# Recurrent stage of a hybrid decoder layer on one core: two of five token chunks stored in the other half of the partitions, their products issued in pairs over all four quarters of the array

## The chip, the core and the metric

The kernel runs on 1 core of one Trainium2 chip. The metric is the device time in microseconds (us). Before the change it is 2426.48 us, the median of 3 runs (2426.11 to 2426.84).

## What is computed

One inference step of one decoder layer in fp32, for a prompt of 256 tokens and 8 samples of 8 tokens (320 tokens in all), width 2048. Three branches work side by side (a recurrent "RWKV-7" mixing, a gated spatial mixing, an attention over a memory), are merged by gates, and a gated MLP follows. The change touches the recurrent branch alone. For each of 16 heads of 64 channels the reference runs, token by token:

```
def step(S, inp):
    r_t, w_t, k_t, v_t, av_t, bv_t = inp
    sa = jnp.einsum('bhvk,bhk->bhv', S, av_t)
    S = S * w_t[:, :, None, :] + sa[..., None] * bv_t[:, :, None, :] + v_t[..., None] * k_t[:, :, None, :]
    return S, jnp.einsum('bhvk,bhk->bhv', S, r_t)
S, ys = lax.scan(step, wkv0.astype(f32), seq)
```

Then the output of each head is normalised, a bonus term is added, and the sum is multiplied by a gate.

## The kernel before

TensorE (PE) spends nearly all of its time on dense products with weights: for each unit of 1 MB of weights, ScalarE (ACT) makes a rounded copy (`hi_unit`, L211), VectorE (DVE) the rest (`lo_unit`, L218), and PE multiplies both with the 320 tokens (`pe_group_steps`, L246, L247, L255). SyncE brings in the units.

The recurrence is computed in chunks of 64 tokens: chunks 0 to 3 are the prompt, chunk 4 (`NCK`) holds the 8 samples. `wkv_pe`, `wkv_dve` and `wkv_act` loop 8 times (two calls of 4 iterations), and each iteration handles two heads: head 0 in partitions 0 to 63, head 1 in partitions 64 to 127. Such an iteration is a chain of small products with names in the table `PR`: `A`, `B`, `Cb`, `Bk`, `Ck` (chunk by chunk products of tokens with tokens), `beT`, `vT`, `kaT`, `alT` (a chunk turned so that its tokens lie in the partitions), `A2` to `QT4` (powers of a triangular matrix), `Z0` to `Z3` (their application), `X4`, `G`, `S0` to `S4`, `X` (states of the chunks), and the output `y` in bank 6. Each name gets one of three PSUM banks in turn (`RING = (4, 5, 7)`), so a product waits in `begin` until the result three names before it has been moved out. DVE moves most of them (semaphore `ring_out`), ACT the turned ones (`turned_out`).

A product of a chunk is two fp32 matmuls of 64x64, one for each head, from `heads`: head h reads partitions 64h to 64h+63 and writes the same ones, so it uses one diagonal quarter of the 128x128 array. The trace shows each fp32 matmul as two records. Tokens in the partitions always lie in the half of their head.

The dense products of the gates and of the branches are cut into 48 steps of 6 matmuls per iteration, and a table `STEPS` says how many are issued in front of which small product: they cover the time in which DVE and ACT work on the result before. `"A": 8` puts 8 steps in front of `A`, `Y_STEPS = 3` more stand in front of `y`. `UNIT_END` tells ACT after which product a weight unit has been used up.

DVE works in program order. `Prog.do` makes it wait for the end of each of its own instructions. Its order in an iteration is: masks on `A` to `Cb`, copies and sums for `A2` to `Z3`, `prepare_logs` (four instructions for the next iteration), `X4`, `G`, the products `sam` and `vtm` (with `m_e8`), the states (`state(c)`, L970), parts of the branches (`branch`, L1783 and L1787), the normalisation of the next iteration's keys (a reciprocal, L833), the copy of `y` (L989), the output's normalisation, and between them six `lo_unit`.

Of the kernel before, what the change touches and what calls it, by code (L numbers as in the profile page):

```python
# [35 lines left out]
CH = 64  # L36
# [72 lines left out]
def hybrid_step(nc, A, O):  # L109
    ctx = ExitStack()  # L110
    with ctx:
# [600 lines left out]
        st_ = [qr[:, 1920 + 64 * c:1984 + 64 * c] for c in range(NCK)]  # L712
# [49 lines left out]
        def wkv_pool(pool, pp):  # L762
# [53 lines left out]
        def prepare_logs(dve, vv, j):  # L816

            dve.wait_ge(S("low_out"), 2 * j + 2)
            vv.do(dve.tensor_scalar(ldx, ldx, -0.5 * C_DECAY, -0.5 * C_DECAY, ALU.mult, ALU.add))
            vv.do(dve.tensor_tensor_scan(cum, m_sc[:, :], ldx, 0.0, ALU.mult, ALU.add))  # L820
            vv.do(dve.tensor_tensor(ldx, cum, ldx, ALU.subtract), "logs")
            vv.do(dve.tensor_scalar(av, av, 0.5, 0.5, ALU.mult, ALU.add))
# [33 lines left out]
        def wkv_start_dve(dve, vv, beside):  # L856
# [13 lines left out]
            prepare_logs(dve, vv, 0)  # L870
            beside.due(AT_STEP["wq"] + 8)
# [21 lines left out]
        def wkv_dve(dve, vv, n):  # L893
            u = U_BR[n]
            with vv.loop(4 * n, 4 * n + 4, PER_V) as i:
# [12 lines left out]
                def masked(o, name, m, sem="ring_out"):  # L908
                    ps(name)
                    m = m[:, :, :] if len(m.shape) == 3 else bmid(m[:, :], NC)  # L910
                    tt(c5(o), c5(pbank(name)[:, 0:T]), m, ALU.mult, sem)

# [15 lines left out]
                tt(c5(t_bo)[:, 0:NCK], c5(pbank("B")[:, 0:T])[:, 0:NCK], bmid(m_bo[:, :], NCK), ALU.mult, "ring_out")  # L928
                ps("beT")
                vv.do(dve.tensor_copy(zc3[:, :, 0:64], c5(pbank("beT")[:, 0:T])), "ring_out")  # L930
                ps("Cb")
                tt(zc3[:, :, 64:128], c5(pbank("Cb")[:, 0:T]), m_in[:, :, :], ALU.mult, "ring_out")
# [3 lines left out]
                masked(t_bk, "Bk", m_st)  # L936
# [3 lines left out]
                masked(t_ck, "Ck", m_in)  # L940
# [27 lines left out]
                def state(c):  # L968
                    ps(f"S{c}")
                    vv.do(dve.tensor_scalar(st_[c], pbank(f"S{c}")[:, 0:64], pend_p[:, c:c + 1], None, ALU.mult), "ring_out")  # L970

                state(0)
                prepare_k(dve, vv, i + 1)
                state(1)
                branch(0, 0)
                state(2)
# [4 lines left out]
                state(3)  # L981
                branch(0, 1)
                ps("X")
                tt(t_x[:, 64:TP], t_x[:, 64:TP], pbank("X")[:, 0:192], ALU.add, "ring_out")
# [33 lines left out]
        PER_V = {"dve": 23, "kk_sq": 1, "logs": 1, "ring_out": N_OUT, "rk_ready": 1, "ops_ready": 1,  # L1018
# [7 lines left out]
        def prepare_act(act, aa, j, ps=None, beside=None):  # L1026
# [3 lines left out]
            if ps:  # L1030
                i = j - 1
                for name, dst, n in (("vT", v_t, T), ("kaT", ka_t, T), ("s0t", qr[:, 896:1408], 512), ("alT", alp_t, 192)):
                    ps(name)
                    aa.do(act.activation(dst[:, 0:n], pbank(name)[:, 0:n], ACT.Copy), "turned_out")
# [36 lines left out]
        def wkv_act(act, aa, n):  # L1071
            with aa.loop(4 * n, 4 * n + 4, {"low_out": 2, "exps": 3, "kk_root": 1, "v_copied": 1, "gn_sqrt": 1, "turned_out": N_OUT_A}) as i:
# [37 lines left out]
        def wkv_pe(pe, n):  # L1110
            u, t = U_BR[n], T_BR[n]
            for i in range(4 * n, 4 * n + 4):
# [18 lines left out]
                def begin(name, *needs):  # L1131

                    p = PR[name]
                    assert p == done[0], name
                    for _ in range(STEPS.get(p, 0) - (Y_STEPS if name == "g" else 0)):
# [40 lines left out]
                def turned(name, src, chunks=range(NC)):  # L1176
                    o = begin(name)
                    for n, c in enumerate(chunks):
                        for h in range(2):
                            r = slice(64 * h, 64 * h + 64)  # L1180
                            last = pe.matmul(o[r, 64 * n:64 * n + 64], src[r, 64 * c:64 * c + 64], m_id[r, :], start=True, stop=True)  # L1181
                    end(last)
# [25 lines left out]
                each("B", be, alp)  # L1208
                turned("beT", be)
                each("Cb", be, rh)  # L1210
                each("A2", t_bd, t_ad, ("Cb",))
                each("B2", t_ad, t_bd)
                each("Bk", ka, alp)
                wait("v_copied", i + 1)
                turned("vT", v_)
                each("RT1", t_b2, t_rt, ("B2",))
                each("B4", t_a2, t_b2)
                each("Ck", ka, rh)
                turned("kaT", ka)
# [14 lines left out]
                turned("alT", alp, range(1, NCK))  # L1234
# [13 lines left out]
                o = begin("G", "Z3")  # L1248
                for c in range(1, NCK):
                    last = heads(ch(o, c - 1), [(ch(alp_t, c - 1), zb(c))])  # L1250
                end(last)

                def state(c):
                    o = begin(f"S{c}", f"S{c - 1}" if c else "G")
                    end(heads(o[:, 0:64], [(zb(c), ch(t_x, c)), (ch(ka_t, c), ch(v_t, c))] + ([(ch(step_, c - 1), st_[c - 1])] if c else [])))

                state(0)
                state(1)
                state(2)
                o = begin("S4")  # L1260
                wait("sam_ready", i + 1)
                end(heads(o[:, :], [(zb(NCK), sam.rearrange("p b v -> p (b v)")), (ch(ka_t, NCK), vtm.rearrange("p b v -> p (b v)"))]))
                state(3)
                o = begin("X", "S2")
                for c in range(1, NCK):
                    last = heads(ch(o, c - 1), [(ch(alp, c), st_[c - 1])])
                end(last)
                for _ in range(Y_STEPS):
                    next(steps, None)
                wait("ring_out", OUT0 + N_OUT * i + 1 + OUT["X"])  # L1270
                wait("gated_out", i + 1)
                for c in range(NC):
                    terms = [(ch(t_x, c), zcb(c)), (ch(v_t, c), ch(t_ck, c))]
                    if 0 < c < NCK:
                        terms.append((st_[c - 1], ch(rh, c)))
# [1289 lines left out]
```

## Time and profile before

| what | value |
|---|---|
| median of 3 runs | 2426.48 us |
| span of the profiled execution, first to last instruction | 2425.4 us |
| instructions in it | 48608 |
| PE busy | 2375.4 us (98%) |
| PE weight loads busy | 2272.1 us (94%) |
| DVE busy | 1467.3 us (60%) |
| ACT busy | 893.6 us (37%) |
| GpSimd busy | 130.5 us (5%) |
| mean granted TensorE clock | 0.996 of full speed |

The profiled execution's own time is its span of 2425.4 us and some 1.1 us around it, which gives the median. Engines overlap, so their busy times don't add up. A matmul's record lasts from its start to the landing of its result, and records overlap: how long a product holds PE is read from the start of one product to the start of the next. The granted clock is 1.00 in all stretches of the recurrent stage, which is 2.4 GHz.

### The profile page before, as it was taken

Reading aid. Unit: us, or ns where it says so; the run is one execution under the profiler, and the core shown is the slowest. Engines: PE = TensorE matmul, PEld = TensorE weight load, DVE = VectorE, ACT = ScalarE, POOL = GpSimd, SP = SyncE. Lnnn points to the kernel's source line nnn. Section 1 sums busy time; section 2 is a strip of 40 time slices with the busy share of each in tenths; the row PEclk is TensorE's granted clock in tenths of the full one; section 3 lists DMA queues with packets and bytes.
Section 4 is the critical chain, followed back from the end, with each engine's and each line's share of the span. In section 5 each row is a group of like instructions: output and inputs, shape, how many; then the busy total and the mean of one; then the engine's idle time right before and its main releaser. Section 6 shows DMA issues by size and latency. Waiting matters only on the chain.

```text
span 2425.4 us, 48608 instructions
## 1 busy us (share of the span) xinstructions
PE 2375.4 (98%) x19598; PEld 2272.1 (94%) x19598; DVE 1467.3 (60%) x2060; ACT 893.6 (37%) x1038; POOL 130.5 (5%) x200
## 2 busy tenths in 40 slices
PE   8999999999999999999999998999999999999998
PEld 6899999898988888888999988999999999999998
DVE  5645444555677666776544446666666666566576
ACT  6433344343333333332434344333333333333334
POOL 3000001000000010000000011000000000000003
PEclk9999999999999999999999999999999999999999
DMA  7544486342333233322444632444444444444443
GB/s 266 192 155 152 152 292 238 103 140 84 96 99 95 92 126 100 97 87 93 143 149 151 201 121 88 157 155 138 156 156 142 152 154 140 143 159 148 156 139 109
DMA packets 282189, 346.67 MB, mean 143 GB/s; under 512 B 6957, under 2 KB 240733, under 8 KB 280907
## 3 DMA queue, kind: packets, MB, share of 16 engines
q1 hardware_dynamic: 272315, 308.44, 39.1%
q0 software_dynamic: 9712, 36.30, 4.6%
q8 instruction: 104, 1.70, 0.3%
q14 instruction: 26, 0.21, 0.0%
q10 hardware_dynamic: 32, 0.01, 0.0%
HBM read 333.83 MB, written 10.89 MB: 142 GB/s over the span
## 4 chain that ended last, share of the span: by engine, by line
PE 86%; DVE 8%; issue 3%; ACT 2%; DMA 1%; DVEq 0%; SPq 0%; ACTq 0%
PE bank L246 20%; PE bank L255 20%; PE bank L247 20%; PE bank L1165 5%; PE bank L227 4%; PE bank L228 4%; PE bank L229 4%; DVE work L906 1%; ACT hi L211 1%; DVE lo L218 1%; PE bank L1181 1%; PE bank L511 1%; DVE q L833 1%; PE bank L512 1%; PE bank L518 1%
## 5 line engine op out<-in xcount | busy, mean ns | idle before, releaser
L218 DVE TENSOR_TENSOR lo<-raw,hi 128x2048 fp32r<-128x2048 f32 x286 | 655.8, 2293 | 505.9 <-ACT hi L211 479.7
L246 PE MATMUL bank<-ah,hi 128*128 128x320 f32 x3200 | 958.1, 313 | 0.2 <-DVE al L532 0.2
L247 PE MATMUL bank<-al,hi 128*128 128x320 f32 x3200 | 945.8, 309 | 0.0
L211 ACT ACTIVATE hi<-raw 128x2048 fp32r<-128x2048 f32 x286 | 548.0, 1916 | 926.3 <-PE bank L255 678.6
L246 PEld LDWEIGHTS bank<-ah,hi 128*128 128x128 f32 x3200 | 600.8, 188 | 13.1 <-issue 9.8
L247 PEld LDWEIGHTS bank<-al,hi 128*128 128x128 f32 x3200 | 601.1, 188 | 0.4
L255 PE MATMUL bank<-ah,lo 128*128 128x320 f32 x3200 | 547.5, 311 | 0.0
L255 PEld LDWEIGHTS bank<-ah,lo 128*128 128x128 f32 x3200 | 487.2, 188 | 4.0 <-issue 0.8
L227 PE MATMUL bank<-bh,hi 128*128 128x320 f32 x704 | 218.7, 311 | 0.2 <-DVE work L2279 0.2
L229 PE MATMUL bank<-bh,lo 128*128 128x320 f32 x704 | 217.5, 309 | 0.0
L228 PE MATMUL bank<-bl,hi 128*128 128x320 f32 x704 | 217.5, 309 | 0.0
L1165 PE MATMUL bank<-work 64*64 64x64 f32 (+2 forms) x3680 | 166.0, 236 | 5.4 <-DVE work L906 4.3
L1165 PEld LDWEIGHTS bank<-work 64*64 64x64 f32 x3680 | 134.0, 134 | 35.8 <-issue 24.6
L227 PEld LDWEIGHTS bank<-bh,hi 128*128 128x128 f32 x704 | 132.2, 188 | 0.6 <-issue 0.6
L228 PEld LDWEIGHTS bank<-bl,hi 128*128 128x128 f32 x704 | 132.2, 188 | 0.0
L229 PEld LDWEIGHTS bank<-bh,lo 128*128 128x128 f32 x704 | 132.1, 188 | 0.0
L2279 DVE TENSOR_TENSOR work<-work,bank 128x320 f32<-128x320 f32 x176 | 85.6, 487 | 56.7 <-PE bank L229 47.1
L246 PE MATMUL bank<-bh,hi 128*128 128x320 f32 x384 | 118.0, 320 | 0.0
L2253 DVE SCALAR_TENSOR_TENSOR rw<-rw,prm 128x336 f32<-128x336 f32 x176 | 100.2, 569 | 22.2 <-DVE rw L2251 1.4
L247 PE MATMUL bank<-bl,hi 128*128 128x320 f32 x384 | 113.6, 309 | 0.0
L906 DVE TENSOR_TENSOR work<-work,bank 128x512 f32<-128x512 f32 (+3 forms) x56 | 28.9, 517 | 97.6 <-PE bank L1165 95.7
L246 PEld LDWEIGHTS bank<-bh,hi 128*128 128x128 f32 x384 | 72.1, 188 | 2.3
(372 smaller groups left out, 2036.2 us busy)
## 6 DMA issues: line engine op xcount, KB each, us to landing
raw<-in_w_in SPq DMA_DIRECT2D x98, 1024.0 KB, 5.2
raw<-in_w_up SPq DMA_DIRECT2D x88, 1024.0 KB, 5.1
raw<-in_w_down SPq DMA_DIRECT2D x44, 1024.0 KB, 5.1
raw<-in_w_branch SPq DMA_DIRECT2D x24, 1024.0 KB, 5.4
raw<-in_w_out SPq DMA_DIRECT2D x16, 1024.0 KB, 5.6
raw<-in_w_mem_k SPq DMA_DIRECT2D x8, 1024.0 KB, 5.6
raw<-in_w_mem_v SPq DMA_DIRECT2D x8, 1024.0 KB, 5.2
work<-in_cache_mem_k POOLq DMA_DIRECT2D x8, 1024.0 KB, 6.7
```

Source lines behind the costliest of these rows:

```text
L211: act.activation(hi[c % NS][:, :], raw[c % 2][:, :], ACT.Copy).then_inc(S("hi_done"), 1)
L218: dve.tensor_tensor(lo[c % NS][:, :], raw[c % 2][:, :], hi[c % NS][:, :], ALU.subtract)\
L227: pe.matmul(out, a_hi, b_hi, start=first, stop=False)
L228: pe.matmul(out, a_hi, b_lo, start=False, stop=False)
L229: return pe.matmul(out, a_lo, b_hi, start=False, stop=last)
L246: pe.matmul(out, w, xh[:, 8 * h + k, :], start=h + k == 0, stop=False)
L247: pe.matmul(out, w, xl[:, 8 * h + k, :], start=False, stop=False)
L255: last = pe.matmul(out, w, xh[:, 8 * h + k, :], start=False, stop=h == units - 1 and k == 7)
L906: vv.do(dve.tensor_tensor(o, a, b, op), sem)
L1165: last = pe.matmul(out[r, :], a[r, :], b[r, :], start=start and m == 0, stop=stop and m == len(pairs) - 1, **kw)
L2253: vv.do(dve.scalar_tensor_tensor(out=o, in0=x, scalar=w, in1=o, op0=ALU.mult, op1=ALU.add), "gate_conv" if j == 2 and q % 8 == 3 else None)
L2279: dve.tensor_tensor(f, f, bank[b][:, 0:T], ALU.add).then_inc(S(f"tile_out{b}"), 1)
```

## The change

It does these things, all inside the iteration of the recurrent stage:

- Chunks 0 and 1 (`TURNED`) keep tokens that lie in the partitions in the other head's half: head h has them in partitions 64(1-h) to 64(1-h)+63. A product that makes such a chunk reads head h's half and writes the other one, which is an off-diagonal quarter of the array. Chunks 2 to 4 (`UPRIGHT`) stay.
- Two products that don't depend on each other get two banks, one for the turned chunks and one for the upright ones, and are issued chunk by chunk in turn (`both`): `A` with `B` (`ABt`, `ABs`), `beT` with `Cb` (`beCt`, `beCs`), `Bk` with `Ck` (`BCt`, `BCs`), `vT` with `kaT` (`vkt`, `vks`).
- The states' two products that don't depend on the state before, and `G`, become one pair of banks, `St` and `Ss`. `S0` goes; `S1` to `S3` keep one product each, and DVE adds the rest, which it has stored scaled in `st_`. `X` gives its first chunk to a new `X1`.
- The terms of `y` for chunks 0 and 1 are issued between the halves of `S4`, whose matmuls are on the diagonal quarters.
- `alT` makes chunks 2 and 3 first, then 4 steps of dense work, then chunk 1, directly ahead of `Z2`.
- `bonus` comes first in the iteration. `prepare_logs` is cut in two (`prepare_shifted`), and `X4` stands ahead of it. The table `STEPS` names other products, with the same sum of 48.
- DVE moves each pair bank by bank. It issues 10 instructions more per iteration, ACT 2 more. PE has as many matmuls as before.

The diff, cut to its core:

```
+        TURNED = (0, 1)
+        UPRIGHT = (2, 3, 4)
-        for _n in ["A", "bonus", "B", "beT", "Cb", "A2", "B2", "Bk", "vT", "RT1", "B4", "Ck", "kaT", "RT2", "s0t",
-                   "Q", "QT", "Z0", "Z0s", "Q2", "QT2", "XB", "Z1", "QT4", "alT", "Z2", "z", "za", "ssq", "Z3", "X4", "G",
-                   "S0", "S1", "S2", "S4", "S3", "X", "g", "mean", "trp", "var", "tr0", "tr1"]:
+        for _n in ["bonus", "ABt", "ABs", "beCt", "beCs", "A2", "B2", "BCt", "BCs", "RT1", "B4", "vkt", "vks", "RT2", "s0t",
+                   "Q", "QT", "Z0", "Z0s", "Q2", "QT2", "XB", "Z1", "QT4", "alT", "Z2", "z", "za", "ssq", "Z3", "X4", "St", "Ss",
+                   "S1", "X1", "S2", "S4", "S3", "X", "g", "mean", "trp", "var", "tr0", "tr1"]:
...
-        STEPS = {"A": 8, "A2": 3, "RT1": 3, "RT2": 3, "Q": 3, "XB": 3, "Z2": 4, "Z3": 4, "S0": 2, "S1": 2, "S2": 2, "S3": 1, "X": 2,
+        STEPS = {"bonus": 8, "A2": 3, "RT1": 3, "RT2": 3, "Q": 3, "XB": 3, "alT": 4, "Z3": 4, "S1": 3, "S2": 3, "S3": 3,
                  "g": 5, "mean": 2, "var": 1}
-        Y_STEPS = 3
+        HELD = {"alT": 4, "g": 3}
...
-                masked(t_ad, "A", m_ad)
+                def part(o, name, at, chunks, m, sem=None):
+                    k = len(chunks)
+                    m = m[:, chunks[0]:chunks[0] + k, :] if len(m.shape) == 3 else bmid(m[:, :], k)
+                    tt(c5(o)[:, chunks[0]:chunks[0] + k], c3(pbank(name)[:, at:at + 64 * k]), m, ALU.mult, sem)
                 ps("bonus")
                 tt(bon, pbank("bonus")[:, 0:T], row_(i + 16), ALU.mult, "ring_out")
-                masked(t_bd, "B", m_bd, None)
...
+                for name, cs in (("ABt", TURNED), ("ABs", UPRIGHT)):
+                    k, states = 64 * len(cs), tuple(c for c in cs if c < NCK)
+                    ps(name)
+                    part(t_ad, name, 0, cs, m_ad)
+                    part(t_bd, name, k, cs, m_bd)
+                    part(t_bo, name, k, states, m_bo, "ring_out")
...
                 plus(zc, "Z3", 512)
-                prepare_logs(dve, vv, i + 1)
                 ps("X4")
                 tt(t_x[:, TP:T], t_x[:, TP:T], pbank("X4")[:, 0:64], ALU.add, "ring_out")
-                ps("G")
-                tt(c3(step_), c3(pbank("G")[:, 0:192]), bmid(m_id[:, :], NCK - 1), ALU.add, "ring_out")
+                prepare_logs(dve, vv, i + 1)
+                ps("St")
+                tt(c3(st_all[:, 0:128]), c3(pbank("St")[:, 0:128]), bc(pend_p[:, 0:2], CH), ALU.mult)
+                tt(step_[:, 0:64], pbank("St")[:, 128:192], m_id[:, :], ALU.add, "ring_out")
+                ps("Ss")
+                tt(c3(st_all[:, 128:256]), c3(pbank("Ss")[:, 0:128]), bc(pend_p[:, 2:4], CH), ALU.mult)
+                tt(c3(step_[:, 64:192]), c3(pbank("Ss")[:, 128:256]), bmid(m_id[:, :], 2), ALU.add, "ring_out")
+                prepare_shifted(dve, vv, i + 1)
...
+                def into_chunk(o, a, b, c):
+                    for h in range(2):
+                        last = pe.matmul(o[half(h ^ (c in TURNED)), :], a[half(h), :], b[half(h), :], start=True, stop=True)
+                    return last
...
+                def both(turned, upright, a1, b1, a2, b2):
+                    t, s = begin(turned), begin(upright, ahead=1)
...
+                    one(s, a1, b1, 2, 0)
+                    one(t, a1, b1, 0, 0)
+                    one(s, a1, b1, 3, 1)
+                    one(t, a1, b1, 1, 1)
+                    one(s, a1, b1, 4, 2)
+                    one(t, a2, b2, 0, 2)
+                    one(s, a2, b2, 2, 3)
+                    end(one(t, a2, b2, 1, 3))
+                    one(s, a2, b2, 3, 4)
+                    end(one(s, a2, b2, 4, 5))
...
+                y_terms(0, 0, start=True)
+                heads(o[:, :], [(zb(NCK), sam_)], stop=False)
+                y_terms(0, 1)
+                y_terms(1, 0)
+                y_terms(1, 1)
+                end(heads(o[:, :], [(ch(ka_t, NCK), vtm_)], start=False))
```

Where the order of instructions moves, it is shown from the built programs. First PE at the start of an iteration; the rows name the PSUM bank that is written and what is multiplied, `ops_ready`, `rk_ready` and `ring_out` are semaphores of DVE, `turned_out` of ACT. Before:

```order
L255 MATMUL bank3<-ah,lo0 128x320 x8
L1165 MATMUL bank4<-work 64x64 [waits ops_ready,turned_out,ring_out]
L1165 MATMUL bank4<-work 64x64 x9
L1207 MATMUL bank5<-work,head_ones 128x320 [waits rk_ready,turned_out,ring_out]
L1165 MATMUL bank7<-work 64x64 [waits turned_out,ring_out]
L1165 MATMUL bank7<-work 64x64 x9
L1181 MATMUL bank4<-m_id,work 64x64 [waits ring_out]
L1181 MATMUL bank4<-m_id,work 64x64 x9
L1165 MATMUL bank5<-work 64x64 [waits ring_out]
L1165 MATMUL bank5<-work 64x64 x9
```

With the change:

```order
L255 MATMUL bank3<-ah,lo0 128x320 x8
L1256 MATMUL bank4<-work,head_ones 128x320 [waits rk_ready,turned_out,ring_out]
L1208 MATMUL bank7<-work 64x64 [waits turned_out,ring_out,ops_ready]
L1208 MATMUL bank7<-work 64x64
L1208 MATMUL bank5<-work 64x64 x2
L1208 MATMUL bank7<-work 64x64 x2
L1208 MATMUL bank5<-work 64x64 x2
L1208 MATMUL bank7<-work 64x64 x2
L1208 MATMUL bank5<-work 64x64 x2
L1208 MATMUL bank7<-work 64x64 x2
L1208 MATMUL bank5<-work 64x64 x2
L1208 MATMUL bank7<-work 64x64 x4
L1208 MATMUL bank5<-m_id,work 64x64 [waits ring_out]
L1208 MATMUL bank5<-m_id,work 64x64
L1208 MATMUL bank4<-m_id,work 64x64 x2
```

`bonus` (with `head_ones`) has moved to the front, and the second pair, which writes banks 5 and 4, waits for `ring_out`: its bank 5 is that of `ABt`, from the pair before it.

Then DVE around the first states; `bank7` with 128x512 is the sum of `Z3`, the two rows with `m_e8` are `sam` and `vtm`. Before:

```order
L906 TENSOR_TENSOR work<-work,bank7 128x512 [waits wkv_ps]
L819 TENSOR_SCALAR work<-work 128x320 [waits low_out]
L820 SCALAR_TENSOR_TENSOR work<-m_scan,work 128x320 [waits dve]
L821 TENSOR_TENSOR work<-work 128x320 [waits dve]
L822 TENSOR_SCALAR rw<-rw 128x320 [waits logs]
L906 TENSOR_TENSOR work<-work,bank4 128x64 [waits wkv_ps]
L906 TENSOR_TENSOR work<-bank5,m_id 128x192 [waits wkv_ps]
L906 TENSOR_TENSOR work<-work,m_e8 128x512 [waits turned_out]
L906 TENSOR_TENSOR work<-work,m_e8 128x512 [waits dve]
L970 TENSOR_SCALAR q<-bank7,q 128x64 [waits wkv_ps]
L827 TENSOR_SCALAR rw<-rw,prm 128x320
```

With the change:

```order
L913 TENSOR_TENSOR work<-work,bank7 128x512 [waits wkv_ps]
L913 TENSOR_TENSOR work<-work,bank4 128x64 [waits wkv_ps]
L823 TENSOR_SCALAR work<-work 128x320 [waits low_out]
L824 SCALAR_TENSOR_TENSOR work<-m_scan,work 128x320 [waits dve]
L913 TENSOR_TENSOR q<-bank5,q 128x128 [waits wkv_ps]
L913 TENSOR_TENSOR work<-bank5,m_id 128x64 [waits dve]
L913 TENSOR_TENSOR q<-bank7,q 128x128 [waits wkv_ps]
L913 TENSOR_TENSOR work<-bank7,m_id 128x128 [waits dve]
L827 TENSOR_TENSOR work<-work 128x320 [waits ring_out]
L828 TENSOR_SCALAR rw<-rw 128x320 [waits logs]
L913 TENSOR_TENSOR work<-work,m_e8 128x512 [waits turned_out]
L913 TENSOR_TENSOR work<-work,m_e8 128x512 [waits dve]
L989 SCALAR_TENSOR_TENSOR q<-bank4,q 128x64 [waits wkv_ps]
L913 TENSOR_TENSOR work<-work,bank5 128x64 [waits wkv_ps]
L833 TENSOR_SCALAR rw<-rw,prm 128x320
```

`X4` has moved ahead of the logs, the one row on `G` has become four on `St` and `Ss`, and the row of `X1` (bank 5, 128x64) follows the state of chunk 1.

## Rows read from the trace of the kernel before

**Rows 1.** The page, its head and first part: busy us (share of the span) xinstructions.

```profile
span 2425.4 us, 48608 instructions
PE 2375.4 (98%) x19598; PEld 2272.1 (94%) x19598; DVE 1467.3 (60%) x2060; ACT 893.6 (37%) x1038; POOL 130.5 (5%) x200
```

**Rows 2.** Busy time of the recurrent stage: PE, PEld, DVE, ACT, POOL, clock.

```profile
551.00:1162.00 611.00, 600.59 (x7604) 539.02 (x7603) 408.98 (x639) 198.38 (x224) 41.33 (x73) 1.00 0.31 96
```

**Rows 3.** The chain of waits, in time order: start us, us, what.

```profile
770.76 0.50 DVE work L906
771.39 0.78 PE bank L1298 x2
```

**Rows 4.** Timeline of PE: start us, us, line, out<-in, records, idle before and its releaser.

```profile
703.68 0.80 PE L1165 MATMUL bank<-work 64*64 64x64 f32 x20
...
710.12 1.97 PE L1165 MATMUL bank<-work 64*64 64x64 f32 x60
711.92 0.75 PE L1181 MATMUL bank<-m_id,work 64*64 64x64 f32 x20
...
715.44 1.96 PE L1165 MATMUL bank<-work 64*64 64x64 f32 x60
...
744.41 1.10 PE L1165 MATMUL bank<-q 64*64 64x64 f32 x32
745.36 0.56 PE L1165 MATMUL bank<-work 64*64 64x64 f32 x12
...
748.42 0.45 PE L1165 MATMUL bank<-work 64*64 64x64 f32 x8 [0.54 <-DVE work L906]
...
750.76 0.45 PE L1165 MATMUL bank<-work 64*64 64x64 f32 x8
...
766.96 0.81 PE L1284 MATMUL bank<-q 128*128 128x320 f32 x2
...
780.02 0.80 PE L1165 MATMUL bank<-work 64*64 64x64 f32 x20
```

**Rows 5.** Groups of PE by line, a line with column tiles of 32: busy us, mean ns.

```profile
L1703 PE MATMUL bank<-work,small 128*32 128x256 f32 x128 | 8.7, 385 | 0.0
```

**Rows 6.** Timeline of PE, two products that lie in different rows of the array.

```profile
738.37 0.53 PE L1239 MATMUL bank<-q 64*128 64x320 f32 x1
738.38 0.53 PE L1241 MATMUL bank<-q 64*128 64x320 f32 x1
```

**Rows 7.** Timeline of DVE, from the sum of Z3 to the copy of y.

```profile
744.62 0.69 DVE L906 TENSOR_TENSOR work<-work,bank 128x512 f32<-128x512 f32 x1 [2.54 <-PE bank L1165]
...
747.66 0.22 DVE L906 TENSOR_TENSOR work<-work,bank 128x64 f32<-128x64 f32 x1
748.01 0.36 DVE L906 TENSOR_TENSOR work<-bank,m_id 128x192 f32<-128x192 f32 x1
748.49 1.42 DVE L906 TENSOR_TENSOR work<-work,m_e 128x512 f32<-128x512 f32 x2
...
750.03 0.29 DVE L970 TENSOR_SCALAR q<-bank,q 128x64 f32<-128x64 f32 x1
...
753.82 0.28 DVE L970 TENSOR_SCALAR q<-bank,q 128x64 f32<-128x64 f32 x1 [0.65 <-PE bank L1165]
...
759.65 0.35 DVE L906 TENSOR_TENSOR work<-work,bank 128x192 f32<-128x192 f32 x1
...
766.41 0.49 DVE L989 COPY work<-bank 128x320 f32<-128x320 f32 x1
```

**Rows 8.** Timeline of DVE, the end of the iteration and the first mask of the next.

```profile
779.41 2.29 DVE L218 TENSOR_TENSOR lo<-raw,hi 128x2048 fp32r<-128x2048 f32 x1 [0.19 <-DVE rw L906]
781.61 0.49 DVE L906 TENSOR_TENSOR work<-bank,m_ad 128x320 f32<-128x320 f32 x1
```

**Rows 9.** Timeline of DVE, the copies after A2 and B2, and the sum after RT1.

```profile
710.97 1.10 DVE L915 COPY work<-bank 128x320 f32<-128x320 f32 x2 [1.64 <-PE bank L1165]
...
716.28 0.49 DVE L906 TENSOR_TENSOR work<-work,bank 128x320 f32<-128x320 f32 x1 [1.06 <-PE bank L1165]
```

More of the change, by code:

```diff
@@ L935, in wkv_dve @@
                 plain(t_b2, "B2")
-                masked(t_bk, "Bk", m_st)
+                for name, cs in (("BCt", TURNED), ("BCs", UPRIGHT)):
+                    ps(name)
+                    part(t_bk, name, 0, cs, m_st)
+                    part(t_ck, name, 64 * len(cs), cs, m_in, "ring_out")
                 weights_low(0)
@@ L1174, in each, with half, out_of_chunk, one @@
                     end(last)
[L1176 to L1182, printed above, removed]
+                def half(h):
+                    return slice(64 * h, 64 * h + 64)
+                def into_chunk(o, a, b, c):
+                    for h in range(2):
+                        last = pe.matmul(o[half(h ^ (c in TURNED)), :], a[half(h), :], b[half(h), :], start=True, stop=True)
+                    return last
+                def out_of_chunk(o, a, b, c, start=True, stop=True, **kw):
+                    for h in range(2):
+                        r = half(h ^ (c in TURNED))
+                        last = pe.matmul(o[half(h), :], a[r, :], b[r, :], start=start, stop=stop, **kw)
+                    return last
+                def both(turned, upright, a1, b1, a2, b2):
+                    t, s = begin(turned), begin(upright, ahead=1)
+                    if turned == "ABt":
+                        wait("ops_ready", i + 1)
+                    def one(o, a, b, c, n):
+                        return into_chunk(ch(o, n), ch(a, c), m_id if b is None else ch(b, c), c)
+                    one(s, a1, b1, 2, 0)
[8 more added lines that the diff above has]
+                    end(one(s, a2, b2, 4, 5))
                 def zb(c):
@@ L1233, in wkv_pe @@
                 each("QT4", t_ad, t_bd, ("QT2",), NCK)
-                turned("alT", alp, range(1, NCK))
+                o = begin("alT")
+                into_chunk(ch(o, 1), ch(alp, 2), m_id, 2)
+                into_chunk(ch(o, 2), ch(alp, 3), m_id, 3).then_inc(S("al_upright"), 1)
+                for _ in range(HELD["alT"]):
+                    next(steps, None)
+                wait("al_upright", i + 1)
+                end(into_chunk(ch(o, 0), ch(alp, 1), m_id, 1))
                 apply("Z2", t_bd, range(NCK), "Z1")
@@ L1247, in wkv_pe, with from_zb @@
                 end(heads(o[:, 0:64], [(alm[:, b, :], s0t[:, b, :]) for b in range(NB)]))
[L1248 to L1251, printed above, removed]
+                o_t, o = begin("St", "Z3"), begin("Ss", ahead=1)
+                wait("turned_out", OUT0_A + N_OUT_A * i + 1 + OUT_A["alT"])
+                def from_zb(o, c):
+                    return out_of_chunk(o, zb(c), ch(t_x, c), c, stop=False)
@@ L1267, in wkv_pe @@
                 end(last)
-                for _ in range(Y_STEPS):
+                for _ in range(HELD["g"]):
                     next(steps, None)
                 wait("ring_out", OUT0 + N_OUT * i + 1 + OUT["X"])
[L1271 to L1275, printed above, removed]
-                    heads(ch(bank[6], c), terms, stop=c < NCK, skip_group_check=c == NCK)
+                for c in UPRIGHT:
+                    for m in range(2):
+                        y_terms(c, m)
@@ L1277, in wkv_pe @@
+                for c in range(1, NCK):
+                    heads(ch(bank[6], c), [(st_[c - 1], ch(rh, c))], start=False, stop=False, skip_group_check=True)
                 for b in range(NB):
```

121 lines of the change are left out of this document (74 added, 47 removed).

## Prediction

> **What bounds the kernel now.** I read the page first: PE is busy for 98% of a span of 2425.4 us [rows 1], and for 600.6 of the 611 us in which the eight iterations of the recurrent stage run, at a granted clock of 1.00, so at 2.4 GHz [rows 2]. That looks like a stage in which every matmul saved is time saved. The chain of waits corrects it: in an iteration it runs over DVE from the sum of Z3 on, and returns to PE only at L1298, the product for the variance, which starts at 771.39 us when DVE's square (770.76 + 0.50) has ended [rows 3]. PE waits there for DVE, it waits 0.54 us for the state S0 behind DVE's logs [rows 4], and between these DVE waits only once for PE, 0.65 us in front of the third state [rows 7]. So the second half of an iteration already runs at DVE's pace, and the first half at PE's. An iteration takes 780.02 - 703.68 = 76.34 us [rows 4].
>
> **What a small product costs.** 60 records take 1.97 us and 20 take 0.80 [rows 4], so a record takes (1.97 - 0.80)/40 = 0.029 us, and a chunk's product (two heads, four records) 0.117 us: call it a round. Both heads' quarters work at once in it. Leaving dense work for small products and coming back costs a group of its own: from 748.42 to 750.76 lie 2 rounds and 12 dense matmuls, 2.34 - 0.23 = 2.11 us; from 710.12 to 715.44 lie 20 rounds and 18 dense ones, 5.32 - 2.34 = 2.98 us [rows 4]. So 6 dense matmuls are 0.87 us, and a group costs 2.11 - 12 x 0.145 = 0.37 us beside its rounds.
>
> **Do four quarters work at once?** No row has it. One bound: the pair takes as long as its records one after the other, 10 rounds. The other: turned chunks are hidden wholly beside upright ones, 6 rounds. Column tiles that read the same rows of the array do overlap: 128 records of 128x32 with 256 columns, 0.385 us each, keep PE busy for 8.7 us, 0.068 us each [rows 5]. Tiles in different rows that write the same columns start 0.01 us apart [rows 6]. A turned quarter shares rows with one upright quarter and columns with the other, and both kinds of sharing are shown to be harmless, so I take 6 rounds.
>
> **What PE saves.** Four pairs (AB, beC, BC, vk) at 4 rounds each are 16 rounds; G with the first two products of S0 to S3 is 11 rounds, St with Ss 6; the four terms of y for chunks 0 and 1 lie beside S4. That is 25 rounds, 2.93 us. Separate groups go from 15 to 12, 1.1 us. The wait for S0 goes, 0.54 us. In all some 4.5 us per iteration, 36 us in eight: what the change would bring if PE set the pace.
>
> **What DVE pays, and why it decides.** The second pair needs bank 5, which DVE must have emptied of ABt. In the kernel before, nothing in the first 60 records had such a wait behind late work. Behind the waiting pair stand its own products, 3 dense steps and A2, and everything of the iteration follows. So a loop closes: sum of Z3, DVE without a pause up to the masks of ABt in the next iteration, the pair beC on PE, and on to the next Z3. I sum it, since no iteration can be shorter.
>
> *DVE's part.* From 744.62 [rows 7] to the end of the last `lo_unit`, 779.41 + 2.29 = 781.70 [rows 8], are 37.08 us. Its wait of 0.65 shrinks to the ordinary 0.13 between instructions with a semaphore of PE (747.88 to 748.01) [rows 7]: 36.56. Removed: G, 0.48 (748.01 to 748.49); S0, 0.29 + 0.13; X goes from 192 columns, 0.35, to 128 [rows 7], which I put at 0.29, between 0.22 for 64 and 0.36 for 192. That is 0.96. Added: St 0.29 + 0.22, Ss 0.29 + 0.29, X1 0.22, with three waits of 0.13 and two gaps of 0.03, 1.76. X4 now follows Z3's sum at once: it lands at 744.41 + 1.10 = 745.51 [rows 4], 0.12 later than DVE could take it. Sum 37.48. Then bonus and the three masks of ABt: the first mask starts at 781.61 now [rows 8], 0.09 before the `lo_unit` ends; 0.49 + 0.13 + 3 x 0.29 + 2 x 0.03 = 1.55, less 0.09 is 1.46. DVE's part is 38.94 us. The exponentials of ACT get their logs 1.8 us later, because `prepare_shifted` stands behind Ss; ACT then has a root and a weight unit before DVE's fourth `lo_unit` needs it. I count that as just covered, with some 0.3 us left; if the cover is gone, DVE's part grows by what is late.
>
> *PE's part.* The pair beC, 6 rounds, and the dense steps to A2: 0.70 + 2.98 = 3.68. From A2 to the sum of Z3 it is 744.62 - 710.12 = 34.50 now [rows 4, 7]. BC and vk save 4 rounds each, the third chunk of alT lies beside Z2: 9 rounds, 1.05 less. Two waits are new. BCs needs bank 7 of A2: DVE starts that copy 0.85 us after A2's start and takes 0.49 [rows 9], so with 0.06 for the handover (y copied at 766.90 [rows 7], gate's product at 766.96 [rows 4]) and 0.05 for the weights the bank is free at 1.45, and B2 is through at 1.22: 0.23 lost. vks needs bank 4 of RT1. BC's products end 2.15 us after A2's start and its four masks at 3.64; the `lo_unit` behind them lets go of DVE at 6.05. RT1 itself starts at 5.09, and its sum could start 0.84 us later, at 5.93 (716.28 after 715.44 now [rows 4, 9]); so it runs from 6.05 to 6.54, the bank is free at 6.65 with handover and weights, and PE is through with B4 at 6.31: 0.34 lost. Sum 3.68 + 34.50 - 1.05 + 0.57 = 37.70.
>
> With 0.10 for the handover (0.06 there, 0.13 in rows 3) the loop is 38.94 + 37.70 + 0.10 = 76.74 us, 0.40 more than 76.34. It closes seven times in eight iterations: +2.8 us. Made against the profiled execution (2425.4 us, and 1.1 us around it, equal to the median) this gives 2426.5 + 2.8 = **2429.3 us**. All of PE's 4.5 us per iteration turn up as waits: about 2 us in front of beC, about 3 us in front of the gate's product, which waits for y's copy.
>
> **The rivals.**
> - *Slower: the quarters don't overlap.* If PE can't start records closer than now, 0.029 us on the mean in every row, a pair takes 10 rounds. beC, BC and vk lie in the loop: 12 rounds, 1.40 us, so 1.80 x 7 = 12.6 us, 2439.1 us. It decides from the point where a pair takes more than 7 rounds. For it: no stretch with small products is quicker. Against it: rows 5 and 6. Chance 0.15. The Trainium skill, "TensorE: Matmul & The Clock Gate", section "Wait — 56ns, not 53.3ns?", says that starts never come closer than about 25 ns; an estimate by it is 1.0 us for a pair's 40 records instead of 0.70, and 2435.6 us for the kernel. By that rule and by the mean of the rows alike this speaks against the change; the 0.01 us of rows 6 are single starts, which no mean disproves.
> - *Slower: DVE's or ACT's part is longer.* Ten instructions more, half of them behind a semaphore: 0.05 us more for each, or a fourth `lo_unit` that waits for ACT, make it 0.5 us more per loop: 0.9 x 7 = 6.3, 2432.8 us. Chance 0.20.
> - *Faster: the loop is looser than I count.* If the gaps of DVE shrink where results have long been ready, or waits go that I kept, the loop could be 1.2 us shorter than its sum, 75.5 us: 0.8 x 7 = 5.6 us less than now, 2420.9 us; if DVE were not in the way at all, 2426.5 - 36 = 2390 us. Against it: the rows of DVE leave no pause to take out but the 0.65 us. Chance 0.15.
> - *It doesn't do what it says.* Matmuls are as many as before and the banks of a pair differ, so nothing hinders the interleaving; without it the first rival's time holds, and it is counted there.
>
> **How the numbers follow.** 0.2% is 4.9 us, about what a measurement of this kernel can tell from no change. The forecast, 2421.6 to 2431.3 us, has a chance of 0.50: it is the sum with some 0.3 us of doubt per loop, and 0.7 towards the fast side. Slower has 0.15 + 0.20 = 0.35, faster 0.15. The range is 2420 to 2440 us: down to a loop 0.9 us shorter than now, up to the first rival.
>
> **What would show it.** Right: PE busy falls by some 25 us with the span unchanged; 40 records of a pair take 0.7 to 0.8 us; PE idles some 2 us in front of beC with DVE as releaser and some 3 us in front of the gate's product; DVE has no pause between Z3's sum and the masks but a short one for X4. Wrong: a pair of 1.0 us or more; an iteration under 76 us with DVE pausing for PE in its second half; DVE waiting for ACT's weight unit.

## The result, and the profile after

The changed kernel takes 2442.62 us (median of 4 runs, 2439.18 to 2445.12), the one before 2426.53 us beside it. The ratio is 1.0066, with a 95% interval of 1.0053 to 1.0078: slower by 0.66%, where I had forecast 2429.3 us and no measurable change. It lies above my range of 2420 to 2440.

The page's head and first part, to be held against [rows 1]:

```profile
span 2441.9 us, 48824 instructions
PE 2356.9 (97%) x19598; PEld 2258.5 (92%) x19598; DVE 1479.5 (61%) x2140; ACT 895.5 (37%) x1054; POOL 129.9 (5%) x200
```

The same stretch as [rows 2], with the same columns (busy us of PE, PEld, DVE, ACT and POOL, granted clock, DMA share, GB/s):

```profile
551.00:1162.00 611.00, 570.63 (x7527) 515.11 (x7525) 408.68 (x697) 194.99 (x234) 39.65 (x70) 0.98 0.31 95
```

PE is busy 570.6 us of these 611 instead of 600.6, so the time saved on PE is there. Over the whole span its busy time fell by 18.5 us (2375.4 to 2356.9), where I had named some 25; the slow stretches below lengthen it. What I had not looked for stands in the clock's column: 0.98 instead of 1.00. Over the whole span the mean granted clock is 0.990, against 0.996 before. The stage is where the whole loss arises: the dense stretch that ends it begins 16.6 us later, and the span is 16.5 us longer. Its first row with the change, and before:

```profile
1172.45 0.39 PE L246 MATMUL bank<-ah,hi 128*128 128x320 f32 x1
```

```profile
1155.86 0.39 PE L246 MATMUL bank<-ah,hi 128*128 128x320 f32 x1
```

PE's timeline, answering to [rows 4]: the pair AB, the pair beC behind its wait, A2 with B2, the pairs BC and vk, and the gate's product with dense matmuls behind it.

```profile
705.78 0.92 PE L1208 MATMUL bank<-work 64*64 64x64 f32 x40
708.54 0.51 PE L1208 MATMUL bank<-m_id,work 64*64 64x64 f32 x18 [1.84 <-DVE work L913]
...
712.22 1.38 PE L1191 MATMUL bank<-work 64*64 64x64 f32 x40
713.70 0.91 PE L1208 MATMUL bank<-work 64*64 64x64 f32 x40
...
718.96 0.91 PE L1208 MATMUL bank<-m_id,work 64*64 64x64 f32 x40 [0.20 <-DVE work L913]
...
769.14 1.38 PE L1378 MATMUL bank<-q 128*128 128x320 f32 x2 [2.89 <-DVE work L1010]
...
770.59 0.47 PE L247 MATMUL bank<-bl,hi 128*128 128x320 f32 x1
770.85 0.47 PE L246 MATMUL bank<-bh,hi 128*128 128x320 f32 x1
```

Two things are to be seen. A pair's 40 records take 0.92 us including the last one's own 0.22, so 0.70 from first start to last; 40 records of plain products (712.22) take 1.38. And the gate's product, which took 0.81 us in [rows 4], takes 1.38, with dense matmuls 0.27 us apart behind it instead of 0.15. That is the granted clock at its lower level, 1.2 GHz. These windows (same columns; the clock is the third figure from the right) look behind the gate's product in five of the eight iterations, at the pause in front of it (687.9), and behind the pair beC once (1025.3):

```profile
613.80:617.20 3.40, 3.38 (x20) 2.99 (x21) 2.50 (x7) 0.17 (x1) 0.00 (x0) 1.00 0.92 277
687.90:690.70 2.80, 0.00 (x0) 0.00 (x0) 2.73 (x4) 0.00 (x0) 0.00 (x0) 1.00 0.00 0
690.70:694.10 3.40, 3.32 (x10) 2.93 (x11) 2.44 (x7) 0.00 (x0) 0.00 (x0) 0.50 0.91 281
694.10:697.50 3.40, 3.19 (x19) 2.48 (x19) 1.66 (x4) 1.28 (x1) 0.00 (x0) 0.99 0.09 27
769.20:772.60 3.40, 3.40 (x11) 3.01 (x12) 2.42 (x6) 0.00 (x0) 0.00 (x0) 0.50 0.97 289
926.30:933.00 6.70, 5.88 (x18) 4.94 (x19) 3.26 (x10) 0.08 (x1) 0.00 (x0) 0.50 0.50 157
1025.30:1028.60 3.30, 3.30 (x13) 3.30 (x14) 1.83 (x6) 0.00 (x0) 0.00 (x0) 0.50 0.72 250
1165.20:1168.50 3.30, 3.30 (x10) 2.91 (x11) 2.42 (x6) 0.00 (x0) 0.00 (x0) 0.50 0.94 286
```

PE stands still from 687.9 to 690.7 us, then the clock is at half for 3.4 us and back at full speed. Only the first iteration is spared; in the other seven a stretch at 1.2 GHz follows the gate's pause (one twice as long), and one more follows the pause in front of the pair beC (1025.3). The three not shown (from 847.7, 1008.2 and 1086.7 us) are at 0.50 or 0.51 for 3.4 us too. That is nine times 3.4 us. What one costs: in the first iteration 13.61 us pass from the gate's product to the next pair AB, in the second, with the clock at half, 15.00 us:

```profile
613.82 0.81 PE L1378 MATMUL bank<-q 128*128 128x320 f32 x2 [2.88 <-DVE work L1010]
...
627.43 0.29 PE L1208 MATMUL bank<-work 64*64 64x64 f32 x4
...
690.78 1.43 PE L1378 MATMUL bank<-q 128*128 128x320 f32 x2 [2.89 <-DVE work L1010]
```

15.00 - 13.61 = 1.39 us. On DVE's side it shows in a wait that is not in the forecast: DVE stands 1.56 us for the product of the mean, in the middle of what I had called DVE's part.

```profile
773.87 0.49 DVE L1017 SCALAR_TENSOR_TENSOR work<-bank,work 128x320 f32<-128x320 f32 x1 [1.56 <-PE bank L1380]
```

So there are two theories to tell apart. *The clock:* the loop is as forecast, some 3 to 5 us slower, and nine stretches at 1.2 GHz cost 9 x 1.39 = 12.5 us, because PE's new pauses bring them. *The path:* the loss sits in the stage's own chain (quarters that hold each other up, DVE's longer part), and the clock only goes with it.

### The profile page after: what moved, and what is told of

Read it like the earlier page. It is cut to its first block, busy times and chain, and to the rows that moved or that the text cites. A ratio compares the mean times of both kernels' runs of the same rounds, so it can differ in the third digit from the quotient of the medians.

```text
span 2441.9 us, 48824 instructions
## 1 busy us (share of the span) xinstructions
PE 2356.9 (97%) x19598; PEld 2258.5 (92%) x19598; DVE 1479.5 (61%) x2140; ACT 895.5 (37%) x1054; POOL 129.9 (5%) x200
## 4 chain that ended last, share of the span: by engine, by line
PE 83%; DVE 10%; issue 4%; ACT 1%; DMA 1%; DVEq 0%; SPq 0%; ACTq 0%
PE bank L246 20%; PE bank L247 20%; PE bank L255 19%; PE bank L227 4%; PE bank L228 4%; PE bank L229 4%; PE bank L1191 3%; DVE work L913 3%; PE bank L1208 1%; ACT hi L211 1%; DVE lo L218 1%; PE bank L511 1%; DVE q L839 1%; PE bank L512 1%; PE bank L518 1%
## 5 line engine op out<-in xcount | busy, mean ns | idle before, releaser
L227 PE MATMUL bank<-bh,hi 128*128 128x320 f32 x704 | 218.7, 311 | 0.5 <-DVE work L2373 0.5
L246 PE MATMUL bank<-bh,hi 128*128 128x320 f32 x384 | 124.5, 336 | 0.0
L1191 PE MATMUL bank<-work 64*64 64x64 f32 (+2 forms) x2208 | 105.2, 244 | 0.9
L1191 PEld LDWEIGHTS bank<-work 64*64 64x64 f32 x2208 | 83.5, 134 | 13.9 <-issue 10.0
L913 DVE TENSOR_TENSOR work<-work,bank 128x512 f32<-128x512 f32 (+2 forms) x64 | 30.1, 470 | 87.1 <-PE bank L1191 84.5
```

The costliest lines, as they stand in the source:

```text
L227: pe.matmul(out, a_hi, b_hi, start=first, stop=False)
L246: pe.matmul(out, w, xh[:, 8 * h + k, :], start=h + k == 0, stop=False)
L913: vv.do(dve.tensor_tensor(o, a, b, op), sem)
L1191: last = pe.matmul(out[r, :], a[r, :], b[r, :], start=start and m == 0, stop=stop and m == len(pairs) - 1, **kw)
```

## The experiments

**1. Fill the gate's pause.** Useless matmuls of a dense matmul's shape in front of the gate's product:

```diff
                 o = begin("g")
+                for _ in range(16):
+                    pe.matmul(pbank("X")[:, 0:T], ah[:, 0, 0:P], ah[:, 1, :], start=True, stop=True)
                 wait("y_out", i + 1)
```

> The changed kernel, with 16 products of no use (128x320, the size of a dense matmul, 0.147 us each, 2.35 us together) issued by PE in front of the gate's product, where it pauses for 2.89 us; nothing reads them. Theory (the clock): the granted clock halves for 3.41 us behind that pause in seven of eight iterations, nine stretches in all, each costs about 1.39 us, 12.5 us together, and the pairs and DVE's path cost only the rest. With the pause filled the clock stays at 1.00, an iteration takes about 76.96 us and the kernel about 2430 us (2428 to 2432). Rival (the quarters share something, or DVE's path is longer, and the clock only accompanies it): work was added and nothing taken away, so 2442 us as before, or more.

Measured: 2439.36 us, before 2426.08, ratio 1.0048 (1.0031 to 1.0065). Neither theory's number. The pair beC of one iteration, a window behind it (709.8) and one behind the gate's product (771.4) say why:

```profile
709.26 0.51 PE L1208 MATMUL bank<-m_id,work 64*64 64x64 f32 x18 [1.84 <-DVE work L913]
```

```profile
709.80:713.20 3.40, 3.40 (x30) 3.28 (x23) 2.27 (x7) 0.00 (x0) 0.00 (x0) 0.50 0.80 277
771.40:774.80 3.40, 3.40 (x20) 3.00 (x21) 2.53 (x7) 0.20 (x1) 0.00 (x0) 1.00 0.89 286
```

Behind the filled pause (771.4) the clock stays at 1.00. It now falls behind the other pause instead, the 1.84 us in front of the pair beC, in six of the eight iterations. My expectation had overlooked that a pause of 1.84 us can be enough. Against the same iterations of run 5 below, in which the clock does not fall, one with a stretch behind the pair beC is 1.5 to 1.6 us longer and the one without (984.60 to 1061.76 us, sum of Z3 to sum of Z3) 0.1.

**2. The kernel before, with work taken out.** In the three dense steps ahead of `y`'s terms only the first and the last matmuls are issued:

```diff
+                THIN[0] = True
                 for _ in range(Y_STEPS):
                     next(steps, None)
+                THIN[0] = False
```

> The kernel before, with 16 dense matmuls per iteration left out (the inner ones of the three steps in front of y's terms; the output misses their share). It has no pairs and no new wait. PE then stands about 2.4 us in front of the gate's product, because DVE copies y when it did. Theory (the clock): the clock falls behind that pause as in the changed kernel, in about seven iterations at 1.39 us, so the kernel gets slower although work is gone: about 2436 us (2430 to 2440; the pause is 0.5 us shorter, so some iterations may be spared). Rival: pauses of PE cost nothing beside DVE: 2426.5 us or less.

Measured: 2432.34 us (10 runs, 2430.78 to 2434.59), ratio 1.0026 (1.0017 to 1.0036). Less work, no pair, no new wait, and 6.3 us more. The gate's product of the second iteration, windows behind that of the second and third, and DVE's sum of Z3, once per iteration:

```profile
689.21 0.81 PE L1290 MATMUL bank<-q 128*128 128x320 f32 x2 [2.27 <-DVE work L993]
```

```profile
690.00:693.40 3.40, 3.40 (x14) 3.25 (x13) 1.80 (x5) 0.00 (x0) 0.00 (x0) 0.50 0.83 277
767.00:770.40 3.40, 3.40 (x20) 3.00 (x21) 2.58 (x7) 0.23 (x1) 0.00 (x0) 1.00 0.92 292
```

```profile
666.88 0.69 DVE L910 TENSOR_TENSOR work<-work,bank 128x512 f32<-128x512 f32 x1 [2.54 <-PE bank L1169]
...
744.62 0.69 DVE L910 TENSOR_TENSOR work<-work,bank 128x512 f32<-128x512 f32 x1 [2.54 <-PE bank L1169]
...
820.96 0.69 DVE L910 TENSOR_TENSOR work<-work,bank 128x512 f32<-128x512 f32 x1 [2.54 <-PE bank L1169]
```

A pause of 2.3 us brings the clock down in five of eight iterations, for 6.3/5 = 1.3 us each. And it is the clock, not the missing work: from one sum of Z3 to the next the spared third iteration takes 76.34 us, as in the kernel before, the second, with the stretch in it, 77.74. This shows the price without any part of the change.

**3. Two dense steps moved past the wait.** From behind the pair beC to ahead of it:

```diff
-        STEPS = {"bonus": 8, "A2": 3, "RT1": 3, "RT2": 3, "Q": 3, "XB": 3, "alT": 4, "Z3": 4, "S1": 3, "S2": 3, "S3": 3,
+        STEPS = {"bonus": 8, "beCt": 2, "A2": 1, "RT1": 3, "RT2": 3, "Q": 3, "XB": 3, "alT": 4, "Z3": 4, "S1": 3, "S2": 3, "S3": 3,
```

> The changed kernel, with two of the three dense steps between the pair beC and A2 moved in front of the pair beC, where PE waits 1.83 us for DVE. The gate's pause stays. Theory (the loop over DVE and back, PE's part 37.87 us from beC to Z3): the part behind the wait gets 1.74 us shorter, of which A2's wait for the masks of ABs (1.0 us behind those of ABt) gives some back: 1.1 us less per iteration, 75.9 without the clock's falls. These stay, so 2442.6 - 7 x 1.1 = 2435 us (2432 to 2438). Rival (PE's total work or the clock alone sets the time): no change, 2442 us.

Measured: 2434.11 us (6 runs), ratio 1.0036 (1.0021 to 1.0050), 8.5 us below the changed kernel's. The runs spread from 2428.54 to 2438.79 us, and with them goes the mean clock: 0.992 to 0.993 in the three below 2431 us, 0.988 to 0.990 in the three above 2437 us. The loop itself is read free of that, from the start of the pair BC in two iterations between which the clock did not fall:

```profile
633.26 0.92 PE L1208 MATMUL bank<-work 64*64 64x64 f32 x40 [0.61 <-DVE work L917]
...
709.04 0.92 PE L1208 MATMUL bank<-work 64*64 64x64 f32 x40 [0.61 <-DVE work L917]
```

75.78 us per iteration, where 75.9 were expected and the kernel before needs 76.34. So the loop over DVE and back is what paces an undisturbed iteration.

**4. Another table of dense steps.** The same 48 steps, put where PE would pause:

```diff
-        STEPS = {"bonus": 8, "A2": 3, "RT1": 3, "RT2": 3, "Q": 3, "XB": 3, "alT": 4, "Z3": 4, "S1": 3, "S2": 3, "S3": 3,
-                 "g": 5, "mean": 2, "var": 1}
-        HELD = {"alT": 4, "g": 3}
+        STEPS = {"bonus": 5, "beCt": 4, "B2": 2, "RT1": 3, "vkt": 1, "Q": 1, "Z0s": 1, "XB": 3,
+                 "alT": 4, "ssq": 1, "St": 1, "S1": 3, "S2": 3, "S3": 3, "g": 9, "var": 3, "tr0": 1}
+        HELD = {"alT": 4, "g": 6}
```

> The changed kernel with another table of dense steps, the same 48: taken from the first half of an iteration, where PE's part closes the loop, into the pauses in front of beC, the gate's product and the variance: bonus 5, beCt 4, B2 2, RT1 3, vkt 1, Q 1, Z0s 1, XB 3, alT 4, ssq 1, St 1, S1 to S3 3 each, g 9 (6 of them ahead of y's terms), var 3, tr0 1. Theory: PE pauses for about 5 us per iteration and is busy for the other 72; if the steps lie in its pauses, the loop closes with PE busy throughout, an iteration takes 72 to 73.5 us, the clock stays at 1.00, and the kernel takes 2426.5 - 8 x 3.5 = about 2398 us (2390 to 2408). Rival (quarters that share rows or columns hold each other up, so that PE's work has not shrunk): not below 2420 us.

Measured: **2393.98 us** (2392.23 to 2396.18), ratio 0.9869 (0.9853 to 0.9886): 32 us faster than the kernel before, 49 us faster than the changed one, and the fastest version of this study. The stage is short and PE full (window as above, then the waits of PE in the stage: us in total, times, longest us):

```profile
551.00:1162.00 611.00, 604.36 (x7801) 547.30 (x7800) 439.30 (x726) 215.52 (x251) 40.53 (x71) 1.00 0.34 105
```

```profile
PE bank L1392 <- DVE work L913: 2.9, 8, 0.4
PE bank L1208 <- issue: 2.1, 2, 1.5
PE bank L1191 <- DVE work L913: 1.2, 7, 0.2
```

The changed kernel's waits were these:

```profile
PE bank L1378 <- DVE work L1010: 24.0, 8, 3.3
PE bank L1208 <- DVE work L913: 15.4, 15, 1.9
```

39.4 us of waits have become about 6, and the clock is back at 1.00.

**5. Fill both pauses.** Run 1, and 8 small products in front of the pair beC:

```diff
-                    t, s = begin(turned), begin(upright, ahead=1)
+                    t = begin(turned)
+                    if turned == "beCt":
+                        for c in [0, 1, 2, 3, 0, 1, 2, 3]:
+                            into_chunk(ch(t, c), ch(alp, 0), ch(be, 0), 0)
+                    s = begin(upright, ahead=1)
```

> The first run filled the gate's pause, and the half-clock stretches moved behind the pause in front of the pair beC, at the same price. Here both are filled: 16 products of 128x320 in front of the gate's product as before, and 8 small ones (a chunk's, 0.117 us each, 0.94 us together) in front of the pair beC, into the bank that its turned half overwrites; they start when the bonus bank is free, so that two pauses of about 0.6 us and 0.3 us stay there. Nothing reads them. Theory (the clock): with no pause over 0.8 us left in the stage the clock stays at 1.00, an iteration takes 77.0 us, and the kernel 2430 to 2432 us at the clock of 0.996 that the kernel before has. Rival (the loss is in the stage's own path, or the added work moves the loss a second time): 2438 us or more, with half-clock stretches still in the stage.

Measured: 2430.41 us (11 runs), before 2425.46, ratio 1.0019 (1.0010 to 1.0028). Useless work makes the changed kernel 12 us faster. The stage, and DVE from the sum of Z3 to the last mask of ABt and on to the next sum of Z3:

```profile
551.00:1162.00 611.00, 594.20 (x7964) 538.77 (x7963) 417.99 (x715) 197.31 (x237) 39.58 (x70) 1.00 0.32 97
```

```profile
746.63 0.69 DVE L913 TENSOR_TENSOR work<-work,bank 128x512 f32<-128x512 f32 x1 [1.67 <-PE bank L1191]
...
772.68 0.49 DVE L1017 SCALAR_TENSOR_TENSOR work<-bank,work 128x320 f32<-128x320 f32 x1
...
785.32 0.29 DVE L913 TENSOR_TENSOR work<-bank,m_bo 128x128 f32<-128x128 f32 x1
...
823.55 0.69 DVE L913 TENSOR_TENSOR work<-work,bank 128x512 f32<-128x512 f32 x1 [1.66 <-PE bank L1191]
```

DVE no longer waits for the mean (772.68 stands without an idle time), and an iteration takes 823.55 - 746.63 = 76.92 us.

**6. The better table, all chunks upright.** The same products, order and banks, in two quarters only:

```diff
-                def into_chunk(o, a, b, c):
+                def into_chunk(o, a, b, c, TURNED=()):
-                def out_of_chunk(o, a, b, c, start=True, stop=True, **kw):
+                def out_of_chunk(o, a, b, c, start=True, stop=True, TURNED=(), **kw):
```

> The kernel with the better table of dense steps (2394.0 us, PE busy all the time), with no chunk turned: the same products in the same order and banks, but all in the two upright quarters. Theory (four quarters work at once, a pair's 40 records take 0.65 us instead of ten rounds of 0.117 = 1.17 us): 25 rounds more on PE per iteration at most, 2.9 us, so 75 us per iteration and 2394 + 8 x 2.9 = 2417 us (2413 to 2420); a pair's records take about 1.15 us. Rival (quarters that share rows or columns hold each other up, and the gain of the table is the table's alone): 2394 to 2397 us.

Measured: 2412.83 us, before 2425.46, ratio 0.9946 (0.9931 to 0.9961). 18.9 us are lost by it; I had expected 23, with 25 rounds as the upper end. An undisturbed iteration takes 74.67 us (587.37 to 662.04, sum of Z3 to sum of Z3) against 72.02 in run 4 (584.54 to 656.56), which is 2.65 us or some 22 rounds; eight iterations make 21.2 us. Run 4 loses 2.1 of them again in the two waits marked "issue" above, for which the trace names no releaser. The pair AB of one iteration:

```profile
698.17 1.38 PE L1208 MATMUL bank<-work 64*64 64x64 f32 x40
```

1.38 us against 0.92 in the row at 705.78 above: 0.46 us for the four rounds that the turned chunks are hidden for, 0.115 each.

**7. The kernel before with a better table.** Its own 48 steps, rearranged with the same aim:

```diff
-        STEPS = {"A": 8, "A2": 3, "RT1": 3, "RT2": 3, "Q": 3, "XB": 3, "Z2": 4, "Z3": 4, "S0": 2, "S1": 2, "S2": 2, "S3": 1, "X": 2,
-                 "g": 5, "mean": 2, "var": 1}
+        STEPS = {"A": 8, "A2": 3, "RT1": 4, "Q": 2, "XB": 5, "Z2": 3,
+                 "ssq": 1, "Z3": 4, "X4": 2, "S0": 2, "S1": 1, "S2": 1, "X": 2, "g": 7, "mean": 1, "var": 2}
```

> The kernel before, without the change, with as good a table of its 48 dense steps as I could work out for it: A 8, A2 3, RT1 4, Q 2, XB 5, Z2 3, ssq 1, Z3 4, X4 2, S0 2, S1 1, S2 1, X 2, g 7, mean 1, var 2. Theory: PE pauses 0.9 to 1.0 us per iteration there and pays 15 groups of dense work; both can shrink a little, to about 75 us per iteration, so 2426.1 - 8 x 1.3 = 2416 us (2413 to 2421). With that, of the 32 us of the other table some 10 would be the table's and 22 the quarters'. Rival (the table does it all): 2400 us or less.

Measured: 2414.26 us, ratio 0.9950 (0.9935 to 0.9966). So a better table alone gives 11.2 us, and with it the change gives another 20.3 (2414.26 to 2393.98, two sets of runs whose kernels before differ by 0.6 us). By run 6 nearly all of these 20 are the four quarters' work; the rest of the change is about neutral. The split depends on how good the two tables are. In run 7 all waits of PE in the stage come to 3.7 us, so its table leaves no long pause to fill; that no better one exists is not shown.

## Why the prediction was wrong

By its own steps:

- **"What a small product costs" and "Do four quarters work at once?": right.** I took 6 rounds, 0.70 us, for a pair; it is 0.70 (705.78), and 1.16 with all chunks upright. The first rival, at 10 rounds, is refuted, and with it the rule of the Trainium skill ("TensorE: Matmul & The Clock Gate", section "Wait — 56ns, not 53.3ns?") by which starts never come closer than about 25 ns: here 40 records start within 0.70 us, 0.018 us on the mean. The measurement decides. That PE gains real time is shown by runs 4 and 6.
- **"DVE's part": right.** Forecast 38.94 us; run 5 has 785.32 + 0.29 - 746.63 = 38.98. The second rival, with DVE's part 0.5 longer or a fourth `lo_unit` that waits for ACT, did not occur.
- **"PE's part": short by 0.18.** Forecast 37.70; from the end of that mask to the next sum are 823.55 - 785.61 = 37.94 us, 0.06 of which is handover (the pair beC starts at 785.67), so 37.88. The first piece, beC to A2, is 3.68 us as worked out (708.54 to 712.22). Nearly all of the 0.18 lies between A2 and the product behind the pair vk: 10.42 us (712.22 to 722.64), where the 10.63 of before (710.12 to 720.75) less 8 rounds, with 0.57 for the waits, give 10.26. It is not traced to a single wait. The two bank waits came where I had put them: the pair BC starts 1.48 us after A2 (forecast 1.45, with 0.05 for the weights that no row shows by itself), the pair vk 6.74 (forecast 6.65).
- **The loop: right in kind, a little too short.** This iteration takes 76.92 us against 76.74 forecast. Its 76.34 us of before I had also read from one iteration. All seven loops, from the first sum of Z3 to the eighth, take 535.79 us in the kernel before and 539.27 in run 5 (rows below): 3.5 us more, where I had 2.8. By its medians run 5 is 5.0 us above the kernel before; what lies outside these loops is not traced.
- **"All of PE's 4.5 us per iteration turn up as waits": right in place and size** (about 2 and about 3 us forecast, 1.84 and 2.89 found), **and the step that failed is what I made of it.** I costed these waits at nothing: PE was ahead of DVE, so its idle time seemed free. I had read the granted clock of 1.00 in [rows 2] and carried it over to a kernel in which PE pauses. The pauses bring the clock to 1.2 GHz for 3.4 us at a time, and the slow stretch begins when PE has work again: the gate's product and the mean, for which DVE waits, or the pair beC and A2, which stand in PE's part. Both are in the loop, so most of the 1.7 us by which 3.4 us at half the clock fall behind is paid.

The sum then closes. DVE's first and eighth sum of Z3, and for run 5 the dense stretch behind them: the changed kernel, run 5, the kernel before.

```profile
591.10 0.69 DVE L913 TENSOR_TENSOR work<-work,bank 128x512 f32<-128x512 f32 x1 [1.67 <-PE bank L1191]
...
1142.28 0.69 DVE L913 TENSOR_TENSOR work<-work,bank 128x512 f32<-128x512 f32 x1 [1.67 <-PE bank L1191]
```

```profile
592.68 0.69 DVE L913 TENSOR_TENSOR work<-work,bank 128x512 f32<-128x512 f32 x1 [1.66 <-PE bank L1191]
...
1131.95 0.69 DVE L913 TENSOR_TENSOR work<-work,bank 128x512 f32<-128x512 f32 x1 [1.66 <-PE bank L1191]
...
1160.70 0.39 PE L246 MATMUL bank<-ah,hi 128*128 128x320 f32 x1
```

```profile
591.78 0.69 DVE L906 TENSOR_TENSOR work<-work,bank 128x512 f32<-128x512 f32 x1 [2.54 <-PE bank L1165]
...
1127.57 0.69 DVE L906 TENSOR_TENSOR work<-work,bank 128x512 f32<-128x512 f32 x1 [2.54 <-PE bank L1165]
```

The seven loops last 551.18 us in the changed kernel and 539.27 with both pauses filled. The difference of 11.9 us, for the eight stretches of 3.4 us that lie in them, is 1.49 us each. The ninth lies behind the eighth sum, where the changed kernel needs 30.17 us to the dense stretch and run 5 28.75, so 1.4 us. That makes 13.3 of the 16.6 us for the clock. The other 3.3 are 3.5 for the loops and 0.5 behind them, less 0.7, because the first sum of Z3 comes 0.68 us earlier than before. In whole kernels: 2430.4 us with the pauses filled, 2442.6 with them open.

No rival named the clock. The first rival's time, 2439.1 us, lies close to the result, by another mechanism altogether; a time near a rival's is no evidence for it. The place to see it coming was the trace of before, outside the recurrent stage. Its mean clock over the span is 0.996, and one of the stretches that are missing follows a pause of PE of 1.88 us, in the stage ahead (a row of PE's timeline, then two windows: up to the pause and the stretch behind it):

```profile
472.30 0.44 PE L1664 MATMUL bank<-ident,small 128*128 128x128 f32 x2 [1.88 <-DVE small L1549]
```

```profile
470.00:472.90 2.90, 1.02 (x8) 0.76 (x8) 2.20 (x10) 0.74 (x1) 0.10 (x1) 1.00 0.72 222
473.40:476.70 3.30, 3.30 (x17) 3.30 (x15) 0.48 (x2) 1.82 (x3) 3.30 (x1) 0.50 0.19 64
```

The Trainium skill speaks of this as well, on the same page, "TensorE: Matmul & The Clock Gate", section "HAM oscillation — how this bites in real kernels": PE standing still between groups of matmuls brings the clock down again and again. The traces agree that it does, but not on how long a pause it takes: the page's rule is about longer ones than any here, and by it alone these would have passed as harmless. Pauses of 1.84 us (run 1), 2.3 (run 2) and 2.9 (the changed kernel) were enough in most iterations, and the measurement decides.

I had worked out two such pauses per iteration. With the window at 473.4 this should have been a rival. An estimate from that window: 3.3 us at half the clock hold 1.65 us of work at full clock, so each fall can cost up to 1.65 us where the work behind the pause lies in the loop, and two in each of eight iterations up to 26 us.

## What to carry to other kernels

TensorE's idle time beside the critical path was not free here: time saved there that turned into pauses of two or three microseconds came back in part as stretches at 1.2 GHz, and these lay just behind the wait, where others wait for PE. So a change that saves PE's work can be half a change: put the remaining work where the pauses would be (here the table of dense steps, 49 us between the two placements), and judge the idea only then. When a forecast says "this turns up as a wait", ask what the granted clock does behind it.

## What was not expected of the hardware

- Useless matmuls in two pauses made a kernel 12 us faster (2442.62 to 2430.41), and 128 dense matmuls left out made another 6.3 us slower (2426.08 to 2432.34).
- A pause does not always bring the clock down: 2.88 us in the first iteration of the changed kernel did not, 2.89 in the second did; the same 2.3 us of run 2 did in five of eight. The pause in front of the pair beC did in six of eight iterations of run 1, and in one of eight in the changed kernel. The wider spread of these kernels goes with it: in run 3 the mean clocks of single executions go from 0.993 to 0.988, and their times from 2429 to 2439 us. Exactly when a pause is spared was not tested.
- Filling one of two pauses moves the slow stretches to the other (run 1) and gains 3 us by the medians, where the runs of the two kernels overlap (2435.3 to 2441.2 and 2439.2 to 2445.1 us); filling both gains 12.
- Four quarters of the array, fed in turn from both halves of the rows into both halves of the columns, work beside each other without a loss that shows: 40 fp32 records of 64x64 in 0.70 us, 1.16 in two quarters.
